# Low parts of the first unit's operand and plain tiles on GpSimd, in the feed-forward stages of a two-block transformer kernel

## What is computed

```python
# first block, twice (i = 0, 1)
h = _layer_norm(DN_ALPHA * h + y, ln1_g[i], ln1_b[i])
u = jnp.square(jax.nn.relu(h @ mlp_w1[i])) @ mlp_w2[i]
h = _layer_norm(DN_ALPHA * h + u, ln2_g[i], ln2_b[i])
...
def _swiglu(x, w_gate, w_up, w_down):
    return (jax.nn.silu(x @ w_gate) * (x @ w_up)) @ w_down
...
# second block, twice (l = 0, 1)
x = x + MACARON * _swiglu(_rmsnorm(x, ffn1_norm), ffn1_w_gate, ffn1_w_up, ffn1_w_down)
...
x = x + MACARON * _swiglu(_rmsnorm(x, ffn2_norm), ffn2_w_gate, ffn2_w_up, ffn2_w_down)
```

## Time and profile before

| | |
|---|---|
| median of 3 runs | 3330.74 us (3329.34 to 3331.68) |
| profiled execution, span from the first to the last instruction | 3327.9 us |
| TensorE busy | 3224.8 us, 97% of the span |
| VectorE busy | 2011.6 us, 60% |
| ScalarE busy | 1456.2 us, 44% |
| GpSimd busy | 872.9 us, 26% |
| mean granted TensorE clock | 0.995 of full speed |

### The profile page before, as it was taken

One profiled execution on the slowest core, in us unless ns is written; L12 is line 12 of the kernel. 1 busy time (PEld: TensorE's weight loads), 2 busy tenths in 40 slices (PEclk: granted clock), 3 DMA queues, 4 the chain that ended last, 5 costly groups with the idle time before them and its releaser, 6 DMA issues.

```text
span 3327.9 us, 47776 instructions
## 1 busy us (share of the span) xinstructions
PE 3224.8 (97%) x20089; PEld 2867.4 (86%) x20092; DVE 2011.6 (60%) x3009; ACT 1456.2 (44%) x2244; POOL 872.9 (26%) x401
## 2 busy tenths in 40 slices
PE   8999999999999999999999999999999999999998
PEld 6887889988668899888999788999999998789998
DVE  6568755445866544576747636574766476367646
ACT  4465445443534544454434324453454343235433
POOL 3210033321400233303232430323222323312232
PEclk9999999999999999999999999999999999999999
DMA  4310233331102333323222322332332323223332
GB/s 133 105 50 26 99 98 112 101 119 58 64 26 89 102 114 102 109 71 125 92 85 97 114 81 84 115 102 83 115 102 89 103 83 125 76 89 108 96 96 76
DMA packets 239814, 308.97 MB, mean 93 GB/s; under 512 B 8336, under 2 KB 168096, under 8 KB 239088
## 3 DMA queue, kind: packets, MB, share of 16 engines
q1 hardware_dynamic: 236016, 291.41, 26.8%
q0 software_dynamic: 3584, 14.52, 1.2%
HBM read 303.80 MB, written 2.10 MB: 92 GB/s over the span
## 4 chain that ended last, share of the span: by engine, by line
PE 78%; DVE 16%; ACT 4%; issue 2%; DMA 0%; POOL 0%; DVEq 0%; ACTq 0%; POOLq 0%
PE bank L598 24%; PE bank L600 24%; PE bank L599 24%; DVE wlo L2082 3%; ACT whi L1322 2%; PE bank L979 1%; DVE wraw L2104 1%; DVE xl L2155 1%; PE bank L618 1%; DVE raw_w L2104 1%; PE bank L1261 1%; PE bank L1252 1%; PE bank L1186 0%; DVE st L2113 0%; DVE wkk_o L2899 0%
## 5 line engine op out<-in xcount | busy, mean ns | idle before, releaser
L3140 POOL TENSOR_TENSOR wlo<-wraw,whi 128x1024 fp32r<-128x1024 f32 (+2 forms) x209 | 531.1, 2545 | 1374.3 <-ACT whi L1322 1374.1
L598 PE MATMUL bank<-xh,whi 128*128 128x256 f32 (+1 forms) x2456 | 721.0, 294 | 46.4 <-DVE zt L2277 17.9
L1322 ACT ACTIVATE whi<-wraw 128x1024 fp32r<-128x1024 f32 (+3 forms) x426 | 441.1, 1039 | 678.7 <-PE bank L600 546.2
L600 PE MATMUL bank<-xh,wlo 128*128 128x256 f32 (+1 forms) x2456 | 715.7, 291 | 0.0
L599 PE MATMUL bank<-xl,whi 128*128 128x256 f32 (+1 forms) x2456 | 711.8, 290 | 0.0
L3140 POOL TENSOR_TENSOR wlo<-raw_w,whi 128x1024 fp32r<-128x1024 f32 (+1 forms) x126 | 300.6, 2389 | 867.4 <-ACT whi L1322 867.4
L598 PEld LDWEIGHTS bank<-xh,whi 128*128 128x128 f32 x2456 | 464.5, 189 | 66.8 <-issue 27.1
L598 PE MATMUL bank<-whi,uh_w 128*128 128x512 f32 x1216 | 473.9, 390 | 0.0
L600 PE MATMUL bank<-whi,ul_w 128*128 128x512 f32 x1216 | 473.3, 389 | 0.0
L599 PEld LDWEIGHTS bank<-xl,whi 128*128 128x128 f32 x2456 | 464.5, 189 | 10.2
L599 PE MATMUL bank<-wlo,uh_w 128*128 128x512 f32 x1216 | 473.2, 389 | 0.0
(11 more groups left out here) (392 smaller groups left out, 5009.7 us busy)
## 6 DMA issues: line engine op xcount, KB each, us to landing
wraw<-in_w_in SPq DMA_DIRECT2D x26, 1024.0 KB, 5.1
wraw<-in_ffn_w_down SPq DMA_DIRECT2D x20, 1024.0 KB, 5.0
raw_w<-in_ffn_w_down SPq DMA_DIRECT2D x20, 1024.0 KB, 5.1
raw_w<-in_mlp_w SPq DMA_DIRECT2D x19, 1024.0 KB, 5.1
wraw<-in_mlp_w SPq DMA_DIRECT2D x17, 1024.0 KB, 5.3
wraw<-in_ffn_w_gate SPq DMA_DIRECT2D x32, 512.0 KB, 4.6
raw_w<-in_ffn_w_gate SPq DMA_DIRECT2D x32, 512.0 KB, 4.8
raw_w<-in_ffn_w_up SPq DMA_DIRECT2D x32, 512.0 KB, 4.4
```

The lines of the kernel that those rows point to most:

```text
L598: M.matmul(o, lh, rh, start=start, stop=False, skip_group_check=more)
L600: return M.matmul(o, ll, rh, start=False, stop=stop, skip_group_check=more)
L1322: A.activation(hi, raw, ACT.Copy).then_inc(*k.w_hi.inc(("hi", j)))
L3140: G.tensor_tensor(lo[:, 0:n], raw[:, 0:n], hi[:, 0:n].bitcast(F), ALU.subtract).then_inc(*k.w_lo.inc(("lo", j)))
```

## The change

1. The low part of the late operand and the low parts of the plain tiles go from VectorE to GpSimd: `plain_rest` of the vector program is gone, and a new function `low_parts` of the GpSimd program does the subtractions in one row, each after a wait for its high part. It stands behind GpSimd's handling of the four weight pieces of the plain tiles and ahead of all others of the stage. In all six stages together these are 6 subtractions of 128 x 4 x 256, and 2 x 4 + 4 x 2 = 16 of 128 x 512.
2. In ScalarE's `units` the copy of a bank stands ahead of the piece of side work of the same product, no longer behind it.

```diff
@@ scalar_program, units
             slots.done()
+            product(blocks[i], p)
             if p != 1:
                 next(rest, None)
-            product(blocks[i], p)
             while waiting:
@@ vector_program, units
-    def units(tag, blocks, product, finish, rest=iter(())):
+    def units(tag, blocks, product, finish):
...
-            if p != 1:
-                next(rest, None)
             product(blocks[i], p)
@@ vector_program, mlp (and the same in glu, with two plain tiles)
-            def plain_rest():
-                low_operand(3, s.x32[1])
-                yield
-                for f in range(4):
-                    dve.wait_ge(at("uh", "up", i, f))
-                    V.tensor_tensor(s.ul[:, f, :], s.t[1][PLAIN[f]], s.uh[:, f, :].bitcast(F), ALU.subtract).then_inc(*done.inc(("ul", "up", i, f)))
-                    yield
...
-            units("up", k.blocks["up", i, a], product, finish, iter(()) if q else plain_rest())
+            units("up", k.blocks["up", i, a], product, finish)
@@ gpsimd_program
+    def low_parts(keys):
+
+        w, r = k.wide, rounds["n"]
+        hi, lo = w.x[3]
+        pool.wait_ge(at("operand hi", r, 3))
+        G.tensor_tensor(lo, w.x32[1], hi.bitcast(F), ALU.subtract).then_inc(*done.inc(("operand", r, 3)))
+        for f, key in enumerate(keys):
+            pool.wait_ge(at("uh", *key))
+            G.tensor_tensor(w.ul[:, f, :], w.t[1][PLAIN[f]], w.uh[:, f, :].bitcast(F), ALU.subtract).then_inc(*done.inc(("ul", *key)))
...
             blocks = k.blocks["up", i, a]
+            if q == 0:
+                slots.skip("up", 4)
+                low_parts([("up", i, f) for f in range(4)])
             slots.skip("up")
...
         for q, (a, b) in enumerate(chunks(DFF2 // 128)):
+            if q == 0:
+                slots.skip("glu", 4)
+                low_parts([("g_gate", g, f) for f in range(2)])
             slots.skip("glu")
```

More of the change, by code:

```diff
@@ L2754, in plain @@
                     V.tensor_tensor(t, t, ring.of(key)[:, :], ALU.mult).then_inc(*done.inc(("free", key), ("gated u", g, f)))
[L2756 to L2762, removed]
             if q == 0:
                 fm("glu", [[(part, g, 0), (part, g, 1)] for part in ("g_gate", "g_up")], plain)
-            units("glu", k.blocks["glu", g, a], product, finish, iter(()) if q else plain_rest())
+            units("glu", k.blocks["glu", g, a], product, finish)
             if q == 1:
```

## The result

| | before | changed |
|---|---|---|
| median of 5 and 5 runs, us | 3330.74 (3329.34 to 3334.54) | 3350.58 (3350.34 to 3351.93) |
| ratio to before, 95% interval | | 1.0058 (1.0046 to 1.0070) |
| span of the profiled execution, us | 3327.9 | 3349.3 |
| mean granted clock of TensorE | 0.995 | 0.991 |

The account below looks back on a forecast made before the run. The prediction took TensorE, 97% busy, as the bound, with its costliest waits on VectorE's addition before product 4. It summed 3330.7 + 13.8 (later starts) + 6.0 (clock) = 3350.5 us, with an 8-in-10 range of 3336 to 3358.

Parts of the forecast that it names:

- The mechanism: In first units, SBUF subtractions of VectorE and GpSimd take turns; VectorE's split of product 3's weights takes 2.4 to 2.6 us.
- the rival "worse": GpSimd over 2 us slower on the late operand's strips, or two clock falls in most stages: 3356 to 3362; chance 0.08.
- The later start: Product 4 starts 1.9 us later in each squared-relu stage, 2.5 us in each SwiGLU stage: 13.8 us in all.
- the chain: VectorE, GpSimd and ScalarE steps ahead of product 4: weight sum ends at 414.8, addition starts at 419.4, product 4 at 420.2.
- The clock: Behind TensorE's longer waits, one fall in each of six stages, four more than before, 1.5 us each: 6.0 us.
- No collision: GpSimd's reads of the moved tiles don't hold VectorE up: 4.8 us off, 3325.9, or 3322.9 without clock falls; chance 0.08.
- one turn only: VectorE's weight sum goes ahead of the first plain tile, so a 1.17 us turn falls out: 3341; chance 0.12.
- nothing measurable: Half a turn lost on VectorE and the plain tiles' gain kept: 3325 to 3337; chance 0.06.

## Why the prediction was right

**The mechanism** held in each step that it announced. In all six first units VectorE's split of product 3's weights took 2.57 or 2.58 us (said: 2.4 to 2.6) and the weight sum behind it 2.31 (said: near 2.4). GpSimd's 6 subtractions of line 3200 and 12 of its 16 of line 3203, here as instructions by line (ns min/median/max, first and last start), came at 2.40 us and at 1.79 to 2.29, the latter against the announced 1.9 to 2.4 (the other four took 2.04 to 2.25):

```profile
L3200 POOL TENSOR_TENSOR xl<-u_w,xh x6: 2397/2402/2403, 409.8 to 3022.5; 128x1024 fp32r<-128x1024 f32 x6
...
L3203 POOL TENSOR_TENSOR ul_w<-t_w,uh_w x12: 1786/2032/2287, 412.1 to 3029.9; 128x512 fp32r<-128x512 f32 x12
```

The late operand's four strips of 256 cost GpSimd nothing extra: 2.40 us, as the 2.41 of the earlier trace rows. That was the open price under the rival "worse". TensorE's waits were 3.59 and 4.95 us for 3.7 and 5.1, and at product 7 0.11 us of idle time was left, where I had said about 0.2.

**The later start** was sized 1.0 us too large: 13.8 in the sum, 12.8 measured. Each stage was 0.17 to 0.2 us less late than the chain said (1.72 for 1.9, 2.33 for 2.5). The turns themselves have the predicted lengths to within 0.1 us, and shifted by the 0.73 us between the two marks the chain runs as said: the weight sum ends at 414.75 (said: 414.8), the addition starts at 419.24 (said: 419.4). So this is rounding summed along the chain, with the 0.1 us by which rows of one engine overlap, not a missing step.

**The clock** was sized too small, 6.0 against 8.6 us, by two errors that partly cancel. I took one fall in each stage, six in all and four more than before. The trace has ten in the six first units, eight more, and one fewer elsewhere. And a fall cost 1.2 us in the mean, not 1.5. The 1.5 that I worked out from matmul counts is right for a fall that lies wholly in work, as the kernel with ScalarE's order alone shows (6.1 us for four). What the sum left out is that with such long waits the clock falls before they end: 7.4 of the 34 us at 1.2 GHz lay within the six waits, where they cost nothing.

**The sum** of the two is 21.4 us between the spans, for 19.8 predicted. The medians differ by 19.84, since the median of the changed kernel lies 1.3 us above its profiled span and not the 2.8 us that I added. That 3350.5 and 3350.58 agree to 0.1 us is therefore chance; the terms are right to about 2 us.

**The rivals.** No collision, one turn only, and nothing measurable are each excluded by the 2.57 and 2.31 us above. Nobody waited for a late plain tile. What would have made the prediction wrong, a loss made up later in the stage, did not come (3.6 us behind at the second unit, 3.7 at the end). It did come the other way: in the kernels with the addition first it was a gain that was given back.

**What stays open.** Why one wait is followed by one stretch at 1.2 GHz and a like one by two is not settled. The 6.1 us of the clock in the kernel with ScalarE's order alone rest on two traces set side by side, without a run that fills its waits. That it is reading, and not subtracting, by which GpSimd holds VectorE up is parted by no run here. And no kernel here takes the waits of units 2 to 4 of the SwiGLU stages away.

## What to carry to other kernels

Before work is moved from VectorE to an idle GpSimd, look on both timelines at what runs at that moment. If both read tiles in SBUF, with two inputs on VectorE, their instructions take turns, and a long one on GpSimd adds what is left of it to whatever VectorE does next (2.57 us for 1.22 behind one that was already running, 3.42 behind one that was let in first); work that only writes, or that reads a bank on VectorE, is free of this. Where one instruction lets TensorE go on, issuing it ahead of work that can wait gave nearly 7 us here (3331.26 to 3324.48), while giving the work to the other engine lost 20. And count a longer wait of a busy TensorE twice, once as the wait and once as the clock behind it; a start that is moved forward at one product is worth only what the next waits of the same chain don't take back.

## What the runs showed of the hardware that I had not expected

- GpSimd is let in between two VectorE instructions even when the second of them has nothing to wait for and was queued first: asked at 412.49, let in at 412.86, with VectorE's next one held until the end of it. One collision in the trace before had shown it; it holds at every place seen here.
- In the kernel of the extra subtractions three VectorE instructions in a row took 2.31 or 2.32 us each. GpSimd and VectorE then alternate at about 1.1 us apiece, and VectorE runs at half its pace for as long as GpSimd has work.
- A memset of 128x512 on GpSimd takes 0.53 to 0.56 us (two in 1.12) and doesn't hold VectorE up at all.
- Waits of 3.6 to 5 us in otherwise dense work put the clock of TensorE to between 0.50 and 0.75 over the next 5.6 us, in six of six places. Matmuls on scrap in the wait kept it at 1.00 and were worth 11.7 us, though product 4 started no more than 0.1 us earlier. Much shorter waits can do it too: behind 2.06 us in squared relu it was 0.70, where behind the 1.35 us of before it was 1.00.
- The clock can fall within a wait, before the work begins again: over the six waits of the changed kernel the granted clock was 0.71 to 0.94.
